# Decode work inside the linear layer's scan: split one-pass spreads, q as narrow weights, a new order at the end

## The chip, the cores and the metric

The kernel runs on one NeuronCore of a Trainium2 chip. Time is device microseconds of one launch; a kernel's time is the median of its runs. All arithmetic is in fp32, either by full fp32 products or by products of parts in the one-pass format fp32r.

## The reference

One inference step of a two-layer decoder with 512 prompt tokens and 8 decode sequences of one token each. Layer 0 mixes tokens by gated linear attention, layer 1 by native sparse attention; each is followed by a squared-relu MLP. The change lies in layer 0's mixer. For each of 4 heads (key width 128, value width 256) and, for the prompt, in chunks:

```python
S_new = jnp.exp(b_last[:, :, 0, :, None]) * S + jnp.einsum('bhck,bhcv->bhkv', kc * jnp.exp(b_last - b), vc)
o = o_inter + jnp.einsum('bhij,bhjv->bhiv', a, vc)
...
o = rms_norm(o, g_out).reshape(B, T, GLA_DV_TOT).astype(h.dtype)
return (o * jax.nn.silu(r)) @ w_out, s
```

For a decode sequence b this is: S'[b,h] = decay * S[b,h] + k[b,h] v[b,h] (an outer product), o[b,h] = q[b,h] S'[b,h]; o is normed over its 256 values, gated and projected. The updated states are outputs too.

## The kernel before, in words

Each engine runs its own hand-written sequence and waits on semaphores: TensorE (PE) for products, VectorE (DVE), ScalarE (ACT), GpSimd (POOL), and SyncE (SP) for loads. Activations lie transposed, model dimension on partitions. Dense projections are split products (`split_products`, L2066): weight and activation are each a high part that ACT copies out and a rest that DVE or POOL subtracts, and three fp32r products make one. A plain fp32 product shows as two records in the trace, an fp32r one as one.

After the input projection the scan follows. Its order is the list `GLA_STEPS` (L472), which every engine walks through, each taking the steps that are its own; a digit is the head, for `vb` the decode sequence. For the prompt: `kt` transposes decayed keys, `at` makes the chunk's triangular scores (32 small products, 64 records, after a bf16 product that zeroes the bank), `u` the states' increments (DVE then chains four states), `o` the outputs, `sq` squares them on ACT, `om` takes their mean on PE, `nr` makes root (ACT), reciprocal, two scalings (DVE) and the gate product (POOL, for the last head DVE). `da`, `xp`, `db` make the decay factors of heads 2 and 3 on DVE, ACT and POOL, `xq`, `dq` those of the queries; `st` stores the final prompt state.

Decode work is woven in by `vb`. The 2 x 2 MB of old states lie in the weight ring (`s0`). For sequence b, ACT scales four states by their decay (L1148), PE spreads the 1024 values of b over all 128 partitions by a product with a selector of 8 rows (L2172, two fp32 products of 512 columns), and DVE adds key times spread value to each state (L1607). Ahead of each `vb` but the first PE makes the outputs of the sequence before (`decode_out`, L2112 to L2121): eight fp32 products with a 128x128 piece of the state as weight and q as one moving column (L2118). The results lie in bank 1 of slot 3.

PSUM has four slots of two banks, handed out in the order of the list `product` (`at` and `omd` slot 3, `u` slot 0, `o` slot 1; `kt`, `om` and `vb` slot 2). Who claims a slot waits until the one before in it was read. After the list come the last decode output, the decode squares (L1156, L1157), their mean (`omd`, L2185) and root (L1162), then DVE's last gate product (L1623), the decode scalings (L1627), the decode gate product and the decode rest (L1633), for which the first output product waits; beside this POOL makes rests of output weights (L809) and of heads (L814) as ACT delivers the high parts (`out_weights_high` L1097, `out_high` L1103). POOL also stores the new states, four sequences at a time (L836); SP loads each half of the output weights after that store and after `od_full`.

## Time and profile before

| | us |
|---|---|
| median of 3 runs | 1972.5 (1971.04 to 1978.53) |
| profiled execution | 1968.85, of which the span 1967.1 |
| scan, first `kt` to first output product | 212.7 to 337.5 |
| TensorE busy over the span | 1790.7 (91%) |
| mean granted TensorE clock | 0.946 |

The page shows one execution. The clock is a share of 2.4 GHz; it is 1.0 or 0.5 at a time, and a value between is a mean. In the timelines and the chain, x counts records. The chain of waits is followed back from the last instruction; a piece with an engine and a line is work, a piece with q its sequencer.

### The profile page before, as it was taken

What the parts mean: (1) busy time and instruction counts of PE and PEld (TensorE: products, weight loads), DVE (VectorE), ACT (ScalarE), POOL (GpSimd) and SP (SyncE); (2) the same over time, 40 slices, a digit from 0 to 9 for tenths busy, and PEclk for the clock granted to TensorE, in tenths of its full rate; (3) what the DMA queues carried; (4) which work ended last, traced back from release to release, by engine and by line L of the source; (5) the groups of instructions that cost most, each with busy time, mean ns of one, the idle gap of its engine ahead of it and who ended that gap; (6) DMA issues with size and microseconds to landing.
All of it is one profiled execution on the core that took longest, in us unless ns stands there. A gap on an engine that the chain in (4) does not pass through costs nothing.

```text
span 1967.1 us, 32578 instructions
## 1 busy us (share of the span) xinstructions
PE 1790.7 (91%) x13592; PEld 1626.9 (83%) x13592; DVE 895.2 (46%) x1347; ACT 678.4 (34%) x1131; POOL 446.3 (23%) x381
## 2 busy tenths in 40 slices
PE   4999997999999997999799998898877999999996
PEld 2989876999999997989677786676644999999996
DVE  6051254744444345446622523877422644434343
ACT  3353233332313232323233422777641332313230
POOL 3244224100000002334212221787702100000000
PEclk9999777999999998999899999899987999999998
DMA  4122122223222221241221210001463322222211
GB/s 161 44 86 86 46 85 95 96 87 116 89 87 87 87 87 50 75 143 63 80 92 54 86 54 1 1 1 44 171 258 129 129 86 87 86 87 86 87 44 44
DMA packets 22254, 166.26 MB, mean 85 GB/s; under 512 B 2112, under 2 KB 9840, under 8 KB 12568
## 3 DMA queue, kind: packets, MB, share of 16 engines
q1 hardware_dynamic: 17896, 122.60, 16.7%
q0 software_dynamic: 4208, 41.45, 5.7%
q8 instruction: 120, 1.97, 0.4%
q14 instruction: 30, 0.25, 0.0%
HBM read 154.00 MB, written 10.04 MB: 83 GB/s over the span
## 4 chain that ended last, share of the span: by engine, by line
PE 79%; DVE 9%; ACT 5%; issue 3%; DMA 2%; POOL 1%; ACTq 0%; DVEq 0%; SPq 0%; PEldq 0%; POOLq 0%
PE slot L2066 53%; PE slot L2297 9%; PE slot L2038 2%; PE slot L2280 2%; ACT phase L1374 2%; PE slot L2140 1%; POOL phase L923 1%; DVE normed_x L1485 1%; PE slot L2172 1%; PE slot L2101 1%; DVE phase L1469 1%; PE slot L2426 1%; PE slot L2397 1%; PE slot L2118 1%; PE slot L2382 1%
## 5 line engine op out<-in xcount | busy, mean ns | idle before, releaser
L1198 ACT ACTIVATE w_high<-weights 128x1024 fp32r<-128x1024 f32 x128 | 135.3, 1060 | 258.1 <-PE slot L2066 250.0
L2066 PE MATMUL slot<-h_high,w_high 128*128 128x260 f32 x1024 | 210.5, 287 | 12.1 <-issue 12.1
L2066 PE MATMUL slot<-h_high,w_rest 128*128 128x260 f32 x1024 | 209.0, 286 | 2.8 <-issue 2.8
L2066 PE MATMUL slot<-h_rest,w_high 128*128 128x260 f32 x1024 | 208.8, 286 | 0.0
L2066 PE MATMUL slot<-u_high,w_high 128*128 128x260 f32 x1024 | 206.3, 283 | 0.0
L2066 PE MATMUL slot<-u_rest,w_high 128*128 128x260 f32 x1024 | 206.0, 283 | 0.0
L2066 PE MATMUL slot<-u_high,w_rest 128*128 128x260 f32 x1024 | 205.9, 283 | 0.0
L1665 DVE TENSOR_TENSOR w_rest<-weights,w_high 128x1024 fp32r<-128x1024 f32 x128 | 156.1, 1222 | 31.1 <-ACT w_high L1198 31.1
L2066 PEld LDWEIGHTS slot<-h_high,w_high 128*128 128x128 f32 x1024 | 160.7, 192 | 10.7 <-issue 10.3
L2066 PEld LDWEIGHTS slot<-h_rest,w_high 128*128 128x128 f32 x1024 | 160.5, 192 | 5.7 <-issue 5.7
L2066 PEld LDWEIGHTS slot<-h_high,w_rest 128*128 128x128 f32 x1024 | 160.3, 191 | 0.0
L865 POOL TENSOR_TENSOR pw_rest<-weights,pw_high 128x1024 fp32r<-128x1024 f32 x20 | 48.0, 2401 | 485.7 <-ACT pw_high L1181 469.1
L2066 PEld LDWEIGHTS slot<-u_rest,w_high 128*128 128x128 f32 x1024 | 157.8, 188 | 0.0
L2066 PEld LDWEIGHTS slot<-u_high,w_rest 128*128 128x128 f32 x1024 | 157.8, 188 | 0.0
L2066 PEld LDWEIGHTS slot<-u_high,w_high 128*128 128x128 f32 x1024 | 157.6, 188 | 0.0
L923 POOL TENSOR_SCALAR phase<-phase 128x128 f32<-128x128 f32 (+3 forms) x128 | 140.5, 1115 | 45.0 <-DVE phase L1478 44.9
L1685 DVE TENSOR_TENSOR phase<-phase 128x520 f32<-128x520 f32 x64 | 44.9, 701 | 202.3 <-ACT phase L1229 202.3
L1689 DVE TENSOR_TENSOR phase<-slot,base 128x520 f32<-128x520 f32 x64 | 44.8, 700 | 186.3 <-PE slot L2066 186.3
L1229 ACT ACTIVATE phase<-slot 128x520 f32<-128x520 f32 x64 | 38.8, 607 | 259.4 <-PE slot L2066 259.4
L2297 PE MATMUL slot<-xt_high,w_high 128*128 128x512 f32 x256 | 107.9, 421 | 4.7 <-DVE xt_rest L1799 4.7
L1799 DVE TENSOR_TENSOR xt_rest<-slot,xt_high 128x512 fp32r<-128x512 f32 (+1 forms) x80 | 48.9, 611 | 134.0 <-ACT xt_high L1305 133.2
L2297 PE MATMUL slot<-xt_rest,w_high 128*128 128x512 f32 x256 | 102.0, 398 | 0.0
(370 smaller groups left out, 3804.6 us busy)
## 6 DMA issues: line engine op xcount, KB each, us to landing
weights<-in_wt SPq DMA_DIRECT2D x47, 2048.0 KB, 8.5
weights<-in_state SPq DMA_DIRECT2D x2, 2048.0 KB, 8.6
out<-weights POOLq DMA_DIRECT2D x2, 2048.0 KB, 8.8
weights<-in_w SPq DMA_DIRECT2D x2, 2048.0 KB, 8.8
phase<-in_v_win SPq DMA_DIRECT2D x4, 1024.0 KB
out<-phase SPq DMA_DIRECT2D x6, 512.0 KB, 9.3
phase<-in_x_prompt SPq DMA_DIRECT2D x2, 1024.0 KB, 6.3
weights<-in_k_win SPq DMA_DIRECT2D x2, 1024.0 KB, 7.1
```

The costliest lines, as they stand in the source:

```text
L865: nc.gpsimd.tensor_tensor(pw_part[n % 2][1][:, :, :], ring[:, t % 2, :, 128 * (n % 4):128 * (n % 4) + 128], pw_part[n % 2][0][:, :, :].bit ...
L923: last = nc.gpsimd.tensor_scalar(rows, rows, small[:, 8 * (n % 4) + 6 + a:8 * (n % 4) + 7 + a], None, ALU.mult)
L1198: nc.scalar.activation(w_part[k % 4][0][:, :, :], ring[:, s, :, 128 * (k % 4):128 * (k % 4) + 128], ACT.Copy).then_inc(w_high_ready, 1)
L1374: ins_ = nc.scalar.activation(pst[:, n % PST, a, 0:w], scores[:, a, :], ACT.Exp, scale=HD ** -0.5, bias=small[:, 8 * (n % 4) + a:8 * (n % ...
L1665: nc.vector.tensor_tensor(w_part[k % 4][1][:, :, :], ring[:, s, :, 128 * (k % 4):128 * (k % 4) + 128], w_part[k % 4][0][:, :, :].bitcast(F ...
L1685: nc.vector.tensor_tensor(u, u, u, ALU.mult).then_inc(usq_ready, 1)
L1689: nc.vector.tensor_tensor(halves(gx), tok(ps), halves(rstd_sq), ALU.mult).then_inc(scale_ready, 1)
L1799: nc.vector.tensor_tensor(xt_part[1][:, sp % 2, 0:w], ps[:, 0, 0:w], xt_part[0][:, sp % 2, 0:w].bitcast(F32), ALU.subtract).then_inc(xt_re ...
L2038: last = mm(ps[0:weights(k).shape[1], a, 0:HT], weights(k), moving(k)[:, HT * a:HT * a + HT], start=k == 0, stop=k == chunks - 1)
L2066: last = mm(ps[0:w.shape[2], a, 0:HT], w[:, k, :], m[:, k, HT * a:HT * a + HT], start=k == 0 and w is high and m is x_high, stop=k == DC - ...
L2280: last = nc.tensor.transpose(ps[:, 0, nr * h:nr * h + nr], st2[0:nr, sp % 2, 128 * h:128 * h + 128], ident[0:nr, 0:nr])
L2297: last = mm(psh[:, c, 0:KV * nr], w1_part[wp][:, 8 * half + sp, 128 * c:128 * c + 128], xt_part[xp][:, sp % 2, half:half + KV * nr], start ...
```

## The change

- The spread of decode values: ACT writes the decode values to a buffer `gvd` and then their high part as fp32r to rows 0 to 7 of `gvd_part`, DVE the rest to rows 32 to 39; the selector holds ones for both, is loaded with 40 rows to `sel_in` and copied to fp32r by POOL. `vb` is then two fp32r products with 40 rows of contraction.
- The decode outputs: `qm` holds, for head h and sequence b, an 8-column weight in which only column b is q. A product with the whole 256 columns of state (h, b) adds row b of head h's outputs, in partitions 32h to 32h+7 of the bank, over all eight sequences. That is four fp32 products for a sequence, behind one wait for all its heads. The bank is zeroed by one more bf16 product at the first `at`.
- Since outputs now lie as rows, `dd` copies them out on ACT, `dt` transposes them on PE, ACT copies and squares them, `dm` is their mean, root, reciprocal, scalings and gate product. These steps stand in the list; `omd` and the work behind the list go.
- The order: `vb4` to `vb7` come earlier, ahead of `nr1`, `st2`, `u3` and `sq2`; `dd` follows `om2`, `dt` `nr2`, `dm` `o3`.
- The stores of the new states go from POOL's queue to SP's. POOL gets two memsets at its start.

```diff
--- before.py
+++ after.py
@@ -177,11 +177,16 @@
...
         wgr = carve("wgr", DC * RANK).rearrange("p (c n) -> p c n", n=RANK)
-        sel = carve("sel", NS * 128)[0:NS, :].rearrange("b (s p) -> b s p", s=NS)
+        carve("sel", NS * 128)
...
         osq = carve("osq", 2 * NP).rearrange("p (v t) -> p v t", v=2)
+        qm = carve("qm", GH * NS * NS).rearrange("p (h x) -> p h x", h=GH)
+        od_rows = carve("od_rows", DV)
+        osq_d = carve("osq_d", 2 * GH * NS)
+        rstd_d = carve("rstd_d", GH * NS)
+        gvd = carve("gvd", D)[0:NS, :]
@@ -194,6 +199,9 @@
...
+        sel_part = part("sel_part", at["sel"][0], NS, 128)[0:40, :, :]
+        sel_in = cols("qe", 0, NS * 128)[0:40, :]
+        gvd_part = part("gvd_part", at["gv"][0] + 4 * D, D)
@@ -472,12 +480,11 @@
...
                       "o0 vb1 u1 xq2 dq2 sq0 om0 nr0 vb2 da3 xp3 st1 "
-                      "o1 kt2 at2 db3 vb3 u2 xq3 sq1 om1 nr1 kt3 at3 dq3 vb4 st2 "
-                      "o2 vb5 u3 sq2 om2 nr2 vb6 st3 o3 sq3 om3 vb7 nr3").split()]
+                      "o1 kt2 at2 db3 vb3 u2 xq3 sq1 om1 vb4 nr1 kt3 at3 dq3 vb5 st2 "
+                      "o2 vb6 u3 vb7 sq2 om2 dd0 nr2 dt0 st3 o3 dm0 sq3 om3 nr3").split()]
         for what, n in GLA_STEPS:
-            if what in ("kt", "at", "u", "o", "om", "vb"):
-                product((what, n), {"at": 3, "u": 0, "o": 1}.get(what, 2))
-        product("omd", 3)
+            if what in ("kt", "at", "u", "o", "om", "vb", "dt", "dm"):
+                product((what, n), {"at": 3, "u": 0, "o": 1, "dm": 3}.get(what, 2))
@@ -684,7 +691,7 @@
...
             sp.dma_start(gw2, ins["gw2"]).then_inc(gla_small_in, 16)
-            sp.dma_start(sel.rearrange("b s p -> b (s p)"), ins["sel"]).then_inc(gla_small_in, 16)
+            sp.dma_start(sel_in, ins["sel"]).then_inc(gla_small_in, 16)
@@ -695,6 +702,9 @@
...
             for g in range(2):
+                sp.wait_ge(s0_new, GH * NS // 2 * (g + 1))
+                sp.dma_start(outs[3].rearrange("l b h k v -> k (l b) h v")[:, 4 * g:4 * g + 4, :, :],
+                             s0[:, 4 * g:4 * g + 4, :, :]).then_inc(s0_out[g], 16)
@@ -771,6 +781,8 @@
...
             nc.gpsimd.memset(cols("zerosb", 0, 256), 0.0).then_inc(bf_ready, 1)
+            nc.gpsimd.memset(gvd_part[:, :].bitcast(F32), 0.0).then_inc(bf_ready, 1)
+            nc.gpsimd.memset(cols("qm", 0, GH * NS * NS), 0.0).then_inc(bf_ready, 1)
@@ -800,6 +812,9 @@
...
                 gla_weights_rest(n)
+                if n == 4:
+                    pool.wait_ge(gla_small_in, 48)
+                    nc.gpsimd.tensor_copy(sel_part[:, :, :].rearrange("b s p -> b (s p)"), sel_in).then_inc(bf_ready, 1)
@@ -831,10 +846,6 @@
...
                         out_rest(1)
-                elif what == "vb" and n % 4 == 3:
-                    pool.wait_ge(s0_new, GH * (n + 1))
-                    pool.dma_start(outs[3].rearrange("l b h k v -> k (l b) h v")[:, n - 3:n + 1, :, :],
-                                   s0[:, n - 3:n + 1, :, :]).then_inc(s0_out[n // 4], 16)
@@ -1001,7 +1012,7 @@
...
-            act.wait_ge(bf_ready, 3)
+            act.wait_ge(bf_ready, 5)
@@ -1068,7 +1079,7 @@
...
                 ps, fr = await_product(act, ("gv", n))
-                dst = gv[0:rows, t, 256 * (n // 5):256 * (n // 5) + 256]
+                dst = (gv[:, t, :] if t < TT else gvd)[:, 256 * (n // 5):256 * (n // 5) + 256]
@@ -1086,6 +1097,8 @@
...
                     exps_key(n // 9)
+                elif n == 19:
+                    nc.scalar.activation(gvd_part[0:NS, :], gvd, ACT.Copy).then_inc(gv_ready, 1)
@@ -1103,6 +1116,14 @@
...
+            def root_d():
+                ps, fr = await_product(act, ("dm", 0))
+                nc.scalar.activation(rstd_d, ps[:, 0, 0:GH * NS], ACT.Sqrt, bias=eps_col).then_inc(root_ready, 1)
+                roots[0] += 1
+                act.wait_ge(root_ready, roots[0])
+                act.sem_inc(fr, 1)
@@ -1120,8 +1141,23 @@
...
                     nc.scalar.activation(go[:, 2 * h:2 * h + 2, 0:NP], ps[:, :, :], ACT.Copy).then_inc(go_ready, 1)
-                    act.wait_ge(go_ready, h + 1)
+                    act.wait_ge(go_ready, h + 1 + (h == GH - 1))
                     act.sem_inc(fr, 1)
+                elif what == "dd":
+                    act.wait_ge(od_full, 2)
+                    nc.scalar.activation(od_rows, slot[3][:, 1, 0:DV], ACT.Copy).then_inc(ogd_ready, 1)
+                elif what == "dt":
+                    ps, fr = await_product(act, ("dt", 0))
+                    od = ps[:, 0, 0:DV].rearrange("p (v h x) -> p h v x", v=2, h=GH)[:, :, :, 0:NS]
+                    nc.scalar.activation(go[:, :, NP:T].rearrange("p (h v) b -> p h v b", v=2), od, ACT.Copy)\
+                        .then_inc(go_ready, 1)
+                    nc.scalar.activation(osq_d.rearrange("p (v h b) -> p h v b", v=2, b=NS), od, ACT.Square)\
+                        .then_inc(osq_ready, 1)
+                    act.wait_ge(go_ready, GH)
+                    act.wait_ge(osq_ready, GH)
+                    act.sem_inc(fr, 1)
+                elif what == "dm":
+                    root_d()
@@ -1150,21 +1186,9 @@
...
             out_high(2)
-            act.wait_ge(od_full, 2)
-            od = slot[3][:, 1, 0:DC * NS].rearrange("p (b c) -> p c b", b=NS)
-            nc.scalar.activation(go[:, :, NP:T], od, ACT.Copy).then_inc(go_ready, 1)
-            nc.scalar.activation(osq[:, 0, 0:DC * NS].rearrange("p (c b) -> p c b", b=NS), od, ACT.Square)\
-                .then_inc(osq_ready, 1)
-            ps, fr = await_product(act, "omd")
+            act.wait_ge(ogd_ready, 2)
+            nc.scalar.activation(go_part[0][:, :, NP:T], go[:, :, NP:T], ACT.Copy).then_inc(heads_high_ready, 1)
             out_weights_high(2)
-            act.wait_ge(on_ready, GH)
-            nc.scalar.activation(rstd[:, 0:GH * NS], ps[:, 0, 0:GH * NS], ACT.Sqrt, bias=eps_col).then_inc(root_ready, 1)
-            roots[0] += 1
-            act.wait_ge(root_ready, roots[0])
-            act.sem_inc(fr, 1)
-            act.wait_ge(ogd_ready, 1)
-            nc.scalar.activation(go_part[0][:, :, NP:T], go[:, :, NP:T], ACT.Copy).then_inc(heads_high_ready, 1)
@@ -1587,6 +1611,12 @@
...
                 decay_queries(h)
+            dve.wait_ge(gv_ready, 21)
+            nc.vector.tensor_tensor(gvd_part[32:32 + NS, :], gvd, gvd_part[0:NS, :].bitcast(F32), ALU.subtract)\
+                .then_inc(gv_ready, 1)
+            dve.wait_ge(bf_ready, 5)
+            dve.wait_ge(gz_ready, GH)
+            nc.vector.tensor_copy(qm[:, :, 0:NS * NS:NS + 1], gq[:, :, NP:T]).then_inc(gv_ready, 1)
@@ -1616,19 +1646,19 @@
...
                     last.then_inc(on_ready, 1)
-            scale = rstd[:, 0:GH * NS]
+                elif what == "dm":
+                    reciprocal_root(rstd_d)
+                    by_head = go[:, :, NP:T].rearrange("p (h v) b -> p h v b", v=2)
+                    for v in range(2):
+                        last = nc.vector.scalar_tensor_tensor(by_head[:, :, v, :], by_head[:, :, v, :], P("gla_g")[:, v:v + 1],
+                                                              rstd_d.rearrange("p (h b) -> p h b", b=NS), ALU.mult, ALU.mult)
+                    link(last)
+                    nc.vector.tensor_tensor(go[:, :, NP:T], go[:, :, NP:T], gr[:, :, NP:T], ALU.mult).then_inc(ogd_ready, 1)
...
             nc.vector.tensor_tensor(o_last, o_last, r_last, ALU.mult).then_inc(og_last_ready, 1)
-            reciprocal_root(scale)
-            by_head = go[:, :, NP:T].rearrange("p (h v) b -> p h v b", v=2)
-            for v in range(2):
-                last = nc.vector.scalar_tensor_tensor(by_head[:, :, v, :], by_head[:, :, v, :], P("gla_g")[:, v:v + 1],
-                                                      scale.rearrange("p (h b) -> p h b", b=NS), ALU.mult, ALU.mult)
-            link(last)
-            nc.vector.tensor_tensor(go[:, :, NP:T], go[:, :, NP:T], gr[:, :, NP:T], ALU.mult).then_inc(ogd_ready, 1)
@@ -2106,17 +2136,15 @@
...
-            pe.wait_ge(bf_ready, 3)
-            pe.wait_ge(gv_ready, 20)
+            pe.wait_ge(bf_ready, 6)
+            pe.wait_ge(gv_ready, 23)
...
+                pe.wait_ge(s0_new, GH * b + GH)
                 for h in range(GH):
-                    pe.wait_ge(s0_new, GH * b + h + 1)
-                    for v in range(2):
-                        n = DC * b + 2 * h + v
-                        last = mm(slot[3][:, 1, n:n + 1], s0[:, b, h, 128 * v:128 * v + 128], gq[:, h, NP + b:NP + b + 1],
-                                  start=True, stop=True)
+                    last = mm(slot[3][32 * h:32 * h + NS, 1, 0:DV], qm[:, h, NS * b:NS * b + NS], s0[:, b, h, :],
+                              start=False, stop=b == NS - 1, skip_group_check=True)
@@ -2133,6 +2161,8 @@
...
                     mm(ps[:, 0, :], identb, zerosb, start=True, stop=False, skip_group_check=True)
+                    if h == 0:
+                        mm(ps[:, 1, :], identb, zerosb, start=True, stop=False, skip_group_check=True)
@@ -2169,21 +2199,29 @@
...
                     for a in range(2):
-                        last = mm(ps[:, a, :], sel[:, h, :], gv[0:NS, TT, 512 * a:512 * a + 512], start=True, stop=True)
+                        last = mm(ps[:, a, :], sel_part[:, h, :], gvd_part[0:40, 512 * a:512 * a + 512], start=True, stop=True)
+                    last.then_inc(fu, 1)
+                elif what == "dd":
+                    decode_out(NS - 1)
+                elif what == "dt":
+                    ps, fu = claim(pe, ("dt", 0))
+                    pe.wait_ge(ogd_ready, 1)
+                    for v in range(2):
+                        last = nc.tensor.transpose(ps[:, 0, 128 * v:128 * v + 128], od_rows[:, 128 * v:128 * v + 128], ident)
+                    last.then_inc(fu, 1)
+                elif what == "dm":
+                    pe.wait_ge(osq_ready, GH)
+                    ps, fu = claim(pe, ("dm", 0))
+                    for v in range(2):
+                        last = mm(ps[:, 0, 0:GH * NS], C("mean_v"), osq_d[:, GH * NS * v:GH * NS * v + GH * NS],
+                                  start=v == 0, stop=v == 1)
...
                 elif what == "om":
-                    pe.wait_ge(osq_ready, h + 1)
+                    pe.wait_ge(osq_ready, h + 1 + (h == GH - 1))
...
                     last.then_inc(fu, 1)
-            decode_out(NS - 1)
-            pe.wait_ge(osq_ready, GH + 1)
-            ps, fu = claim(pe, "omd")
-            squares_d = osq[:, 0, 0:DC * NS].rearrange("p (h v b) -> p h v b", v=2, b=NS)
-            for v in range(2):
-                last = mm(ps[:, 0, 0:GH * NS], C("mean_v"), squares_d[:, :, v, :], start=v == 0, stop=v == 1)
-            last.then_inc(fu, 1)
@@ -2560,9 +2598,10 @@
...
     parts.append(np.where(end[None, None, :] <= q[:, :, None], 0, NEG).astype(np.float32).reshape(128, -1))
-    sel = np.zeros((NS, NS, 128), np.float32)
+    sel = np.zeros((40, NS, 128), np.float32)
     sel[np.arange(NS), np.arange(NS)] = 1
-    return np.concatenate(parts, 1), sel.reshape(NS, -1)
+    sel[np.arange(NS) + 32, np.arange(NS)] = 1
+    return np.concatenate(parts, 1), sel.reshape(40, -1)
...
```

## Rows read from the trace of the kernel before

**Rows 1.** The page, its part on the chain that ended last, by engine.
```profile
PE 79%; DVE 9%; ACT 5%; issue 3%; DMA 2%; POOL 1%; ACTq 0%; DVEq 0%; SPq 0%; PEldq 0%; POOLq 0%
```

**Rows 2.** Windows over the scan: length, busy us of each engine, granted clock, DMA share.
```profile
213.00:338.00 125.00, 112.16 (x602) 87.15 (x600) 63.67 (x96) 46.83 (x74) 39.52 (x31) 0.71 0.24 81
```

**Rows 3.** Chain of waits from 205 to 345 us: start us, us, engine, line, records.
```profile
by line: PE slot L2140 18.5%; PE slot L2172 14.9%; PE slot L2118 10.8%; PE slot L2066 10.7%; PE slot L2149 9.1%; PE slot L2160 8.7%; PE slot L2178 6.3%; PE slot L2163 6.1%; DVE phase L1616 4.4%; DVE base L1469 2.6%; PE slot L2129 1.7%; DVE 
...
219.95 3.71 PE slot L2172 x4
...
241.47 1.68 PE slot L2118 x16
243.15 2.15 PE slot L2172 x4
...
248.62 1.72 PE slot L2178 x4
...
278.95 6.88 PE slot L2140 x64
285.83 3.39 PE slot L2118 x16
...
299.36 1.91 PE slot L2172 x4
...
303.19 1.93 PE slot L2178 x4
...
337.48 7.61 PE slot L2066 x51
```

**Rows 4.** Timeline of TensorE, 1441 to 1450 us: start, us, engine, line, operation, tiles.
```profile
1442.09 1.07 PE L2457 MATMUL slot<-phase 128*32 128x512 f32 x8
1443.08 1.97 PE L2426 MATMUL slot<-base,weights 128*128 128x128 f32 x16
```

**Rows 5.** Line L2486: ns min/median/max, first and last start, forms.
```profile
L2486 PE MATMUL slot<-phase x160: 374/379/636, 1476.9 to 1503.8; 128*32 128x256 f32 x128, 63*32 63x256 f32 x16, 8*32 8x256 f32 x16
```

**Rows 6.** Chain of waits over the whole span, products of split parts.
```profile
969.65 2.81 PE slot L2297 x12
```

**Rows 7.** Timeline of ScalarE from 195 to 345 us.
```profile
244.88 1.04 ACT L1126 ACTIVATE phase<-phase 128x1024 f32<-128x1024 f32 x1
...
267.02 0.60 ACT L1112 ACTIVATE normed_x<-slot 128x512 f32<-128x512 f32 x1 [0.18 <-ACT phase L1122]
```

**Rows 8.** Timeline of VectorE from 195 to 345 us; in brackets idle time before.
```profile
219.99 0.69 DVE L1564 TENSOR_TENSOR normed_x<-slot,base 128x512 f32<-128x512 f32 x1 [64.29 <-PE slot L2140]
...
251.39 3.35 DVE L1469 RECIPROCAL base<-base 128x512 f32<-128x512 f32 x1
...
256.11 1.65 DVE L1607 SCALAR_TENSOR_TENSOR weights<-slot,phase,weights 128x256 f32<-128x256 f32 x4
...
303.69 1.51 DVE L1578 SCALAR_TENSOR_TENSOR normed_x<-normed_x,phase,slot 128x256 f32<-128x256 f32 x3
...
328.44 6.11 DVE L1616 SCALAR_TENSOR_TENSOR phase<-phase,base 128x512 f32<-128x512 f32 x2
334.59 1.23 DVE L1623 TENSOR_TENSOR phase<-phase 128x1024 f32<-128x1024 f32 x1
```

**Rows 9.** Timelines of GpSimd (POOL), 0 to 112 and 100 to 345 us.
```profile
63.47 2.40 POOL L790 TENSOR_TENSOR gw_rest<-weights,gw_high 128x1024 fp32r<-128x1024 f32 x1 [3.35 <-ACT gw_high L1014]
...
266.02 6.99 POOL L782 TENSOR_TENSOR phase<-phase 128x64 f32<-128x64 f32 x8 [6.84 <-ACT phase L1052]
...
319.99 0.58 POOL L823 DMA_DIRECT2D out<-normed_x  x1
...
328.70 2.34 POOL L814 TENSOR_TENSOR go_rest<-phase,go_high 128x1024 fp32r<-128x1024 f32 x1
331.00 2.33 POOL L809 TENSOR_TENSOR gw_rest<-weights,go_w_high 128x1024 fp32r<-128x1024 f32 x1
```

**Rows 10.** The page, DMA issues: KB each, us to landing.
```profile
out<-weights POOLq DMA_DIRECT2D x2, 2048.0 KB, 8.8
```

## The prediction

> **What bounds the kernel now.** I read the page's chain first: TensorE (PE) carries 79% of it, so what is worth time is what PE does or waits for [rows 1]. The change touches one stage, the linear layer's scan from 213 to 337.5 us. Its windows show PE at work for 112.2 of 125 us, the granted clock 0.71 on average, so it runs somewhat longer at 1.2 than at 2.4 GHz [rows 2]. The chain of this stage stays on PE from the first `at` to 323 us; then it goes over DVE (the last state update, the last head's norm) until the output projection starts at 337.48 [rows 3]. The reader is to see two different stages: up to `om3` time is TensorE's instructions, behind it none of them.
>
> Two lines of it are what the change attacks: L2118, the decode outputs (16 records a sequence, two for each fp32 product), and L2172, the spread values (4 records). For one sequence they take 1.68 us at full clock and 3.39 at half, and 1.91 and 3.71 [rows 3]. Of the 140 us of that view the first has 10.8%, 15.1 us, and off the chain some 3.5 more for the seventh sequence, hidden beside DVE's update; the second has 14.9%, 20.9 us: 39.5 us in all.
>
> **Prices of the new products.** Decode outputs: 4 products in place of 8, an 8-column weight in place of 128, 256 moving columns, each head in its own quarter of the output's partitions. The nearest rows are 32-column weights with 512 moving columns, four quarters side by side: eight records start at 1442.09, the next wide transposes at 1443.08, so 0.99 us at full clock [rows 4]. Of that 2 x 0.43 is streaming by length; half the columns make 0.43, and with the 0.13 left over 0.56, at half clock 1.0. The wait for the updated state is now one for all four heads, behind which the first three queue; updates of the sequence before are long done. Bounds: nothing on the path where another engine is awaited, and 8 records in turn at 374 to 634 ns of one such record [rows 5], 3.0 to 5.1 us. I take 0.56 and 1.0, since the nearest row has the same four-quarter form.
> Spread values: two products of split parts. Split parts with 512 columns run 12 in 2.81 us [rows 6], 0.234 each, so 0.47, at half clock 0.9. The contraction is 40 rows in place of 8; 8 rows (L2172) and 128 (L2297) stream a column at the same rate, so I charge nothing for it; the other end is the old 1.91. A pair (decode output and spread) is then 1.03 or 1.9, 1.4 at the mean clock, where it was 3.6 to 7.1.
> The Trainium skill (TensorEngine Tiling (Array Packing), Key Properties) says that changing the tiling mode, not just the tile, drains TensorE. The change makes 16 such switches. The trace agrees that a switch costs something, but the 0.13 us above holds both of a visit's two; the rule names no price, and rival 5 has it as a mechanism.
>
> **The sum, in four stretches**, each against the chain before [rows 3].
> A, first `at` to start of `om0` at 248.62. The first spread goes from 3.71 to 0.9: -2.8. The second pair ran 1.68 and 2.15 and would fall to 1.2, but `om0` also needs ScalarE (ACT), which after `o0` copies, scales four states, makes an exponential and squares: it ended 245.92, 4.45 after `o0`'s end at 241.47 [rows 3, 7]. PE would be there 1.2 + 3.3 = 4.5 after it, 3.3 being the state product up to 248.62. No wait yet: -2.65. A: **-5.4**.
> B, `om0`'s end (250.34) to the start of the last `at` (278.95): 28.6. Were PE alone in question, four products less would save 10. But the rows of DVE and ACT show a chain of equal length: root, reciprocal 3.35, scaling, state update (ends 257.8, 7.4 after `om0`) [rows 8], exponents, ACT's exponentials, its copy of `o1`, its copy of `kt2` to 267.62, 17.3 after [rows 7]. Nothing of this moves earlier. PE now meets it three times. `kt2` writes slot 2, which DVE frees at +7.4: PE, there at +6.2, waits 1.2. `vb3` waits for `kt2`'s copy at +17.3, where PE would be at +15. Then 0.7 spread, 2.8 `u2`, 2.7 `om1` (`om0` took 1.72 at full clock; such products double at half, so about 2.7), root 0.7, spread 0.8, to +25.0; and because `vb4` now lies ahead of `kt3` in slot 2, `kt3` waits for its state update, 1.65 [rows 8]: +26.7, transposes and zeroing 0.8: +27.5. B: **-1.1**. POOL's 6.99 us of key decays, done at 273.0 [rows 9], is 22.7 after `om0`, not last.
> C, last `at` to start of `om2` at 303.19: 24.2. Out go 3.39 + 3.71 + 1.68 + 1.91 = 10.7; in come two pairs, 2.8. Then a new wait: `vb7` lies ahead of `om2` in slot 2, DVE does the head's states first (a copy and 1.51, about 2.0) and the update 1.65 after [rows 8], with hand-overs 3.9 after `u3`; the third pair lies inside. C: -10.7 + 2.8 + 3.9 = **-4.0**.
> D, `om2` to the output projection: was 34.3. The last decode products, their squares, mean and root now lie ahead of `o3` and `om3`, so the 6.4 us of the last update pair and the 1.8 us of small decode steps behind the norm leave the end. What is late next is POOL. From `om2`'s start: `om2` 2.7, decode output 0.8, ACT's copy of its rows 0.45 and root 0.75 (4.7); DVE reciprocal and scaling 4.8 (9.5); POOL's product 2.34, three more of 2.34, its store's issue 0.58 (19.4), three more: 7.0 (26.4) [rows 9]. DVE's scaling of the last head needs POOL to stop: in the trace the same two instructions took 6.11 us where two normally take 1.4, because POOL ran without a pause until 333.33; they ended 1.22 after it [rows 8, 9]. So +1.22, product 1.23 [rows 8], decode rest and hand-over 0.5: 29.4. D: **-4.9**. The small decode scalings on DVE are held up by POOL's first burst as well, which ends ahead of the second.
> The Trainium skill (SBUF - State Buffer, SBUF: two separate sides) calls the port pair shared by the two engines an exclusive lock, held by whichever starts first for its whole instruction. The scalings began at 328.44 and were not through before two POOL instructions were, so here DVE waited for more than the one instruction that the rule allows; by the rule it would get in after one, which is the tail rival below.
> Sum: -5.4 - 1.1 - 4.0 - 4.9 = **-15.4 us**.
>
> **What I cost at nothing.** Two more memsets on POOL: it idles from about 1 us until 21. The split of the selector: a POOL copy of at most 2.4 us, in one of the pauses of 3.35 us between weight blocks of 2.40 [rows 9]. 128 KB more for it in front of the weight tiles: under 0.5 us, and weights wait for ACT there. DVE's two small instructions for the split values and the spread-out q lie where it idles 64.29 us [rows 8]. ACT's one (about 1 us of 1024 columns) precedes the gate products, between which it is mostly idle. With no cover each would cost its length, some 4 us together. The states' stores leave POOL's queue for SP's, where they lie ahead of the waits for the output weights' tiles. The second can now start by about 295, its tile lands some 17 us later (twice the 8.8 of the old store [rows 10]), and its first use is the fifth output product, at about 345: hidden.
>
> The profiled execution took 1968.85 us (span 1967.1), 3.65 under the median 1972.5 of runs from 1971.04 to 1978.53. A profile after should show about 1953.5, the median **1957**.
>
> **Rivals.** (1) TensorE's gain arrives whole: 39.5 - 11 = 29 in the scan and 5 behind it, 1939. For it: the chain is nearly all PE. Against it: the three waits of B and the one of C, read from order and rows. (2) The clock. If the shortened, oftener interrupted PE sits at 1.2 GHz for three quarters of the scan rather than a half, its remaining 80 us of work (112 less some 31) grow by about 13, of which the waits swallow half: 1963.5; at a quarter, 1951.5. Low stretches follow the `at` products and waits; but some also follow the one-column products that go. (3) The tail: POOL lets DVE in after one instruction each: the norm ends some 4 us sooner, 1953. (4) The narrow products don't run side by side: 8 x 0.21 = 1.7 us at full clock, as before; it counts where PE is last, 5 of 8 visits: 1963 to 1966. (5) Slower: every record drains before the next and at each switch, 374 to 634 ns a record, mean 5 us with half clock [rows 5]: 8 x 4.2 = 34 over my price, most of it on the path, with 8 of it swallowed by waits: 1983. It turns the sign from a decode output of 2.7 us on (15.4 / 8 over my 0.8). Against it: the 0.99 us for eight records.
>
> **Numbers.** Forecast 0.50 (its own range 1951 to 1962), (1) 0.12, (2) slow side 0.18, (3) 0.10, (4) 0.06, (5) 0.04. Range 1945 to 1966: it holds (2) to (4) and the faster half between forecast and (1). Half a per cent is 9.9 us, about what a measurement of this kernel tells from none. Under 1962.6 lie the forecast, (1), (3) and 0.07 of (2): faster 0.79; same 0.11 + 0.06 = 0.17; slower 0.04.
>
> **What would show it.** A decode output of 0.5 to 1.0 us and a spread of 0.5 to 0.9 on PE; new PE idle ahead of `kt2`, the second state product, `kt3` and the third `om`; the last scalings ending about 1.2 us behind POOL; the output projection starting near 322; everything behind it shifted and unchanged. A narrow product over 2 us, or no waits on PE, would prove me wrong, one on each side.

## The result and the profile after

The changed kernel takes 1940.5 us (median, 1938.35 to 1941.27) beside 1974.9 for the kernel before (1971.04 to 1978.53): ratio 0.9824, 95% interval 0.9801 to 0.9848. I had forecast 1957, at lowest 1945. The gain is 34 us in the medians and 27.9 in the profiled spans (1967.1 to 1939.2), where 15.4 were forecast. The direction was right, the size outside my range. The profiled execution of the kernel before was a quick one (1968.85 us, 6 under the median), so the account by stages below is of the 27.9 us alone.

The chain by engine and the window over the scan answer to [rows 1] and [rows 2].

```profile
PE 78%; DVE 10%; ACT 6%; issue 2%; DMA 2%; POOL 1%; ACTq 0%; DVEq 0%; SPq 0%; PEldq 0%; POOLq 0%
```

```profile
213.00:338.00 125.00, 96.11 (x572) 74.63 (x577) 73.39 (x98) 48.45 (x76) 39.54 (x30) 0.71 0.26 89
```

TensorE is at work 16 us less in that window and the mean granted clock is the same, 0.71. The window hides two things: it holds 8 us of the output projection more, and the clock of a stretch changed though the mean did not. The chain of waits of the changed kernel, 205 to 335 us (start, us, engine, line, records), answers to [rows 3]:

```profile
243.99 2.00 PE slot L2223 x4
...
254.75 9.11 PE slot L2170 x64
263.86 0.97 PE slot L2146 x8
264.84 1.15 PE slot L2202 x2
...
275.85 8.50 PE slot L2170 x64
...
299.80 2.85 PE slot L2223 x4
...
310.21 4.07 DVE phase L1654 x2
314.30 2.30 DVE phase L1657
316.60 3.27 DVE base L1493
319.90 7.64 DVE phase L1646 x2
327.57 1.22 DVE phase L1661
329.07 5.94 PE slot L2096 x26
```

The output projection begins at 329.07 where it began at 337.48: the scan gives 8.4 us, half of the forecast. So the forecast was too large in the stage that it worked out, and nearly 20 us came from places it never looked at. The chain names them. The feed-forward stages have 3072 products on line L2096 (L2066 before). In the changed kernel the chain over the whole span shows each as one unbroken piece:

```profile
381.73 369.11 PE slot L2096 x3072
1549.28 369.13 PE slot L2096 x3072
```

In the kernel before each is broken twice. From its chain of 560 to 780 us:

```profile
559.92 15.00 PE slot L2066 x125
574.91 1.55 issue
576.47 1.58 PE slot L2066 x11
578.04 1.35 issue
579.40 92.53 PE slot L2066 x757
671.93 1.54 issue
```

"issue" is time for which the profile knows no reason: no semaphore, no data. From first to last product these two stages took 378.5 and 383.1 us before and 369.2 and 369.2 after, 23.3 us less. The scan gives 8.4, and 3.8 are given back, 0.9 by a slower start of the output projection and 3.0 by the attention stages: 27.9 in all. These 3.0 I don't take for an effect of the change: the stages from the first feed-forward stage's end to the second's start took 792 to 800 us in all fourteen profiles, in no order that follows an edit.

What differs at those breaks is in the page's table of DMA queues (packets, MB, share), the row for instructions, first the kernel before, then the changed one:

```profile
q8 instruction: 120, 1.97, 0.4%
```

```profile
q8 instruction: 83, 1.36, 0.3%
```

37 packets less, of 16.4 KB each. Asked for 560 to 770 us, the DMA view counts 19 such packets in the kernel before and none in the changed one. The stage's last three panels are a loop in TensorE's program, of 1578 instructions a turn (768 products with a weight load each, and 42 others), with two jumps back per stage; the breaks stand at these jumps. After each jump some 9 of the packets come one after another over the whole next turn, so all of the loop is fetched again. The record of the jump itself is 3.5 to 3.8 us long in the kernel before and 0.2 in the changed one. The four jumps account for 20.9 of the 23.3 us (turns of 95.7 to 98.8 us for 92.3). The other 2.4 lie ahead of the first jump: the first 4 us of the two stages ran at a mean granted clock of 0.67 and 0.63 before and of 1.0 after. That part changes from profile to profile, and stages without a stall take 369.2 to 370.7 us.

The change touches no instruction of the loop. But it makes TensorE's program 153 instructions shorter ahead of it (fp32 products run as two records each, and there are fewer), so the loops lie elsewhere among the 16 KB pieces in which the program is fetched.

The Trainium skill (Runtime: NRT & Kernel Launch, Instruction fetch mechanics) says that instructions are refilled in blocks of 16 KiB, 256 instructions, and that a taken branch whose target is outside "the current 2-page window" forces a fetch and stalls. The trace agrees on the block (16.4 KB a packet) and on the stall, but not on the window: the changed kernel jumps back over six blocks without a fetch. That gave theory P: 1578 is six blocks and 42 instructions, so a turn touches seven blocks or, from 41 of the 256 starting positions, eight. With seven nothing is fetched again; with eight TensorE stalls at each jump.

### The profile page after: what moved, and what is told of

Read it like the earlier page. It is cut to its first block, busy times and chain, and to the rows that moved or that the text cites. A ratio compares the mean times of both kernels' runs of the same rounds, so it can differ in the third digit from the quotient of the medians.

```text
span 1939.2 us, 32429 instructions
## 1 busy us (share of the span) xinstructions
PE 1763.0 (91%) x13510; PEld 1603.5 (83%) x13515; DVE 905.0 (47%) x1349; ACT 679.6 (35%) x1133; POOL 444.8 (23%) x382
## 4 chain that ended last, share of the span: by engine, by line
PE 78%; DVE 10%; ACT 6%; issue 2%; DMA 2%; POOL 1%; ACTq 0%; DVEq 0%; SPq 0%; PEldq 0%; POOLq 0%
PE slot L2096 53%; PE slot L2335 9%; PE slot L2068 2%; PE slot L2318 2%; ACT phase L1398 2%; PE slot L2170 2%; DVE normed_x L1509 1%; POOL phase L934 1%; PE slot L2435 1%; PE slot L2131 1%; PE slot L2464 1%; DVE phase L1493 1%; PE slot L2420 1%; ACT phase L1412 1%; DVE base L1493 1%
## 5 line engine op out<-in xcount | busy, mean ns | idle before, releaser
L2096 PE MATMUL slot<-h_high,w_high 128*128 128x260 f32 x1024 | 206.7, 283 | 0.0
L2096 PE MATMUL slot<-h_high,w_rest 128*128 128x260 f32 x1024 | 206.5, 283 | 0.0
L2096 PE MATMUL slot<-u_high,w_high 128*128 128x260 f32 x1024 | 206.4, 283 | 0.0
L2096 PE MATMUL slot<-h_rest,w_high 128*128 128x260 f32 x1024 | 206.3, 283 | 0.0
L2096 PE MATMUL slot<-u_rest,w_high 128*128 128x260 f32 x1024 | 206.1, 283 | 0.0
L2096 PE MATMUL slot<-u_high,w_rest 128*128 128x260 f32 x1024 | 206.1, 283 | 0.0
L2096 PEld LDWEIGHTS slot<-h_high,w_high 128*128 128x128 f32 x1024 | 157.9, 188 | 0.1
L2096 PEld LDWEIGHTS slot<-h_high,w_rest 128*128 128x128 f32 x1024 | 157.8, 188 | 0.0
L2096 PEld LDWEIGHTS slot<-u_high,w_rest 128*128 128x128 f32 x1024 | 157.8, 188 | 0.0
L2096 PEld LDWEIGHTS slot<-u_rest,w_high 128*128 128x128 f32 x1024 | 157.8, 188 | 0.0
L2096 PEld LDWEIGHTS slot<-u_high,w_high 128*128 128x128 f32 x1024 | 157.6, 188 | 0.0
L2096 PEld LDWEIGHTS slot<-h_rest,w_high 128*128 128x128 f32 x1024 | 157.6, 188 | 0.0
L2335 PE MATMUL slot<-xt_high,w_rest 128*128 128x512 f32 x256 | 101.7, 397 | 0.0
```

The lines of the kernel that those rows point to most:

```text
L2096: last = mm(ps[0:w.shape[2], a, 0:HT], w[:, k, :], m[:, k, HT * a:HT * a + HT], start=k == 0 and w is high and m is x_high, stop=k == DC - ...
L2335: last = mm(psh[:, c, 0:KV * nr], w1_part[wp][:, 8 * half + sp, 128 * c:128 * c + 128], xt_part[xp][:, sp % 2, half:half + KV * nr], start ...
```

## The experiments

Times are medians; each group has its own runs of the kernel before (1970.3, 1972.5, 1970.2 us). "Scan" is first `at` to first product of the output projection; FF0 and FF1 are first to last product of the two feed-forward stages, where 369.2 to 370.7 is a stage without a stall; positions count the kernel's own instructions ahead of each loop, modulo 256.

```
kernel                    us      ratio (95%)             scan   FF0    FF1    positions
before                    1974.9  1                       124.0  378.5  383.1  170 191
after                     1940.5  0.9824 (0.9801-0.9848)  114.7  369.2  369.2   17  38
e1  after + 158 empty     1955.8  0.9914 (0.9881-0.9948)  111.2  380.5  370.3  175 196
e2  after + 220 empty     1950.5  0.9883 (0.9845-0.9922)  112.1  369.2  370.6  237   2
e3  before + 60 empty     1954.0  0.9909 (0.9877-0.9940)  127.2  369.2  369.2  230 251
e4  after + 128 empty     1952.9  0.9888 (0.9847-0.9930)  114.8  369.2  379.0  145 166
e5  before + 5 empty      1962.9  0.9954 (0.9932-0.9975)  127.3  381.5  370.4  175 196
e6  fp32 spreads          1946.9  0.9866 (0.9837-0.9895)  121.9  370.7  370.7   49  70
e7  other slots           1930.4  0.9787 (0.9756-0.9817)  106.7  370.6  369.2   17  38
e8  POOL held back        1933.4  0.9797 (0.9769-0.9826)  111.8  370.7  370.6   17  38
e9  POOL held longer      1932.8  0.9814 (0.9789-0.9839)  106.6  370.4  370.4   17  38
e10 slots and e9          1923.6  0.9767 (0.9741-0.9794)  102.1  370.7  369.2   17  38
e11 e10, earlier burst    1925.5  0.9764 (0.9741-0.9787)   99.9  370.7  370.3   17  38
e12 after + 138 empty     1955.8  one run                 114.7  373.9  381.3  155 176
```

### Where the loops lie: e1 to e5 and e12

All have the same edit, with N = 158, 220, 128, 138 on the changed kernel and 60 and 5 on the kernel before; `idle` is a semaphore that nobody waits for.

```diff
+            for _ in range(N // 2):
+                pe.sem_inc(idle, 1)
             pe.wait_ge(ident_in, 32)
...
             mean_square(0)
+            for _ in range(N - N // 2):
+                pe.sem_inc(idle, 1)
```

e1. 

> The changed kernel with 158 empty instructions (an increment of a semaphore that nobody waits for) put into TensorE's program at two places where TensorE idles in the first 60 us, so that the two loops of the feed-forward stages stand as far into TensorE's program as they did in the kernel before. Theory P (position of the loops): the body of 1578 instructions straddles one 256-instruction page more, is fetched again at each turn, TensorE stalls at four turns, and the 22.8 us that the two feed-forward stages gained go again: stage lengths about 381 and 383 us, time 1963. Rival Q (the stages run faster because of what the scan does differently: clock, memory traffic, buffers): the stages stay at 372 and 369 us, time 1940.

Half of it came. FF0 stalls again at both jumps, FF1 not. From the chain of e1:

```profile
568.05 1.77 issue
...
1559.75 370.02 PE slot L2101 x3072
```

The time also holds 5.5 us by which the scan starts later. I had thought TensorE idle at the two places, but in its records the empty instructions start 0.15 us apart: the first 79 run from 0.8 to 12.8 us, where the first transposes had begun at 7.0, and the other 79 from 28.3 to 40.5. Q is out: the scan of e1 is that of the changed kernel, and FF0 is slow.

e2. 

> As the run before, with 220 empty instructions. Theory P: the loops start shortly behind a page border again, the body fits into seven pages, no stall at the turns: stages of 372 and 369 us, time 1940. Rival R (more instructions ahead of the loops are what brings the stalls, wherever the page borders lie): 1963 or more.

No stall, though it has the most instructions ahead: R is out. The time is not 1940, since the start comes 9.8 us later; that is the padding's own price.

e3. 

> The kernel before, nothing of the change, with 60 empty instructions at the same two idle places. Theory P: the loops slip over a page border, the stalls at the four turns go, time 1974 - 23 = 1951 and the scan as long as before. Rival Q: 1974, both feed-forward stages at 381 and 383 us.

As theory P said (1954.0, both stages 369.2, scan 127.2). This is the kernel before, without its stalls. Beside it the changed kernel is 13.4 us faster in the medians, and 17 by the two ratios, each to its own group's kernel before; e3 starts its scan 2.5 us late by its padding, which has to come off. So without the stalls the change is worth some 11 to 14 us, a little under the 15.4 of the forecast; e3's ten times spread over 22 us (1944.4 to 1966.0), so this can't be said more closely.

e4. 

> The changed kernel with 128 empty instructions. 
e5. 

> The kernel before with five empty instructions in TensorE's program ahead of the loops. Theory P in its sharp form: counted over all runs so far, a loop stalls when it starts at position 166 to 191 of a 256-instruction page (by the count of the kernel's own instructions), and not at 2 to 145 or 196 to 251. Five more put the first loop at 175 (stalls stay, stage about 380 us) and the second at 196 (no stall, 369 us): time 12 us under the kernel before, 1959. Rival: only the rough distance matters, or the layout of other engines' programs: both stages as before, 1971.

Five instructions that do nothing take the stalls out of the second stage (383.1 to 370.4) and leave them in the first (381.5). From the chain of e5:

```profile
578.15 1.53 issue
...
1570.22 370.10 PE slot L2071 x3072
```

The kernel is faster by 9.5 us (ratio 0.9954, interval below 1), less than the 12 expected. In the profile the second stage alone gives 12.7; the scan and the first feed-forward stage were 3 us longer each.

e12. 

> The changed kernel with 138 empty instructions: the first loop starts at position 155 of a page, the second at 176. Theory P says that a body of 1578 instructions (six pages and 42) touches an eighth page for 41 of the 256 positions; the last that stalls lies between 191 and 195 by the runs so far, so the first between 151 and 155: both loops stall, stages of 379 to 383 us each. Rival (another width): the first stage 369 us, as at position 145.

At 176 both jumps stall (381.3). At 155 only the first of two does: its turn takes 96.9 us, the next 92.3, as a free one. So the lower edge lies above 145 and at or near 155, where a width of 41 puts it (the bounds alone allow 37 to 50), and at 155 the outcome is mixed, which theory P does not say. This rests on one run.

### Where the scan's gain went: e6 and e7

The timeline of TensorE in the changed kernel (start, us, line; in brackets idle time and what ended it) shows the new prices and the new waits:

```profile
239.42 0.62 PE L2146 MATMUL slot<-weights,phase 128*8 128x256 f32 x8
239.97 0.73 PE L2202 MATMUL slot<-gvd_part,sel_part 40*128 40x512 f32 x2
...
253.31 1.09 PE L2157 MATMUL slot<-base,phase 128*128 128x128 f32 x4 [2.46 <-DVEq L1640]
254.75 9.11 PE L2170 MATMUL slot<-phase 128*16 128x16 f32 x64 [0.36 <-issue]
...
275.08 0.63 PE L2157 MATMUL slot<-base,phase 128*128 128x128 f32 x4 [1.90 <-DVEq L1640]
275.85 8.50 PE L2170 MATMUL slot<-phase 128*16 128x16 f32 x64
...
299.80 2.85 PE L2223 MATMUL slot<-phase,base 128*128 128x512 f32 x4 [2.93 <-DVEq L1640]
```

The waits are those of the forecast. What it lacks is the line under two of them: the third and fourth `at` took 9.11 and 8.50 us. The fourth took 6.88 before [rows 3], and the third, in the same chain of the kernel before:

```profile
259.53 5.41 PE slot L2140 x64
```

That is 5.41, for the same 64 records. Windows over just these products give the granted clock (the number before the DMA share), in the changed kernel

```profile
254.80:263.80 9.00, 9.00 (x65) 8.56 (x66) 3.26 (x9) 5.40 (x7) 2.45 (x5) 0.50 0.05 16
275.90:284.30 8.40, 8.40 (x67) 7.97 (x70) 3.88 (x3) 2.15 (x5) 2.87 (x2) 0.55 0.72 266
```

and in the kernel before, the third `at` (the fourth ran at 0.74 there):

```profile
259.60:264.90 5.30, 5.30 (x65) 5.00 (x64) 3.14 (x9) 2.13 (x3) 0.00 (x0) 1.00 0.07 25
```

With the new waits ahead of them, the third `at` ran at 1.2 GHz, where it had run at 2.4, and the fourth for nearly all its length, where it had run at 2.4 for about half.

e6.

```diff
-  last = mm(ps[:, a, :], sel_part[:, h, :], gvd_part[0:40, 512 * a:512 * a + 512], ...)
+  last = mm(ps[:, a, :], sel_part[0:NS, h, :].bitcast(F32), gvd[:, 512 * a:512 * a + 512], ...)
```

> The changed kernel with the spread values as before, fp32 products of 8 rows (1.91 us at full clock, 3.7 at half) in place of split ones of 40 rows (0.73 and 1.22). If a spread's price arrives where PE is last: of eight, those of the first head's stretch (2.5) and of om1's, at3's stretch (1.2 to 2.5 each) show in full, those behind a wait for slot 2 only in what exceeds the wait: 7 to 12 us more in the scan, time 1949. Rival (the scan is bound by DVE's and ACT's chain, waits swallow nearly all): 0 to 3 us, 1942.

6.4 us in the medians, 7.2 in the scan: about half of the difference in price (1.25 us at full clock, 2.6 at half, eight times) arrives, the other half is swallowed. The spread was worth its edit.

e7.

```diff
-  product((what, n), {"at": 3, "u": 0, "o": 1, "dm": 3}.get(what, 2))
+  product((what, n), {"at": 3, "u": 0, "o": 1, "dm": 3, "vb": {2: 0, 4: 0, 7: 1}.get(n, 2)}.get(what, 2))
```

> The changed kernel with three of the eight spread values written to other buffers of the accumulator memory (the third and fifth to slot 0, the eighth to slot 1, all others stay in slot 2), nothing else. If the new PE waits ahead of kt2 (2.46 us), kt3 (1.90) and the third om (2.93) are the price of sharing slot 2 with a spread that waits for DVE's update: they go, the third om then waits some 0.3 us for ScalarE, and with less half-clock time behind them the scan is 5 to 7 us shorter, time 1934. Rival (DVE's and ACT's chain of equal length stands behind them): the waits come back ahead of u2, at3 and o3, and the scan gains 0 to 2 us.

10.1 us in the medians (7 by the ratios) and 8.0 in the scan of the profile, more than the high end. Its TensorE timeline:

```profile
250.51 0.60 PE L2157 MATMUL slot<-base,phase 128*128 128x128 f32 x4
...
251.26 5.72 PE L2170 MATMUL slot<-phase 128*16 128x16 f32 x64
...
263.22 1.22 PE L2202 MATMUL slot<-gvd_part,sel_part 40*128 40x512 f32 x2 [5.27 <-ACTq L1136]
...
272.78 6.38 PE L2170 MATMUL slot<-phase 128*16 128x16 f32 x64
...
292.87 1.98 PE L2223 MATMUL slot<-phase,base 128*128 128x512 f32 x4 [0.34 <-ACT phase L1162]
```

The three waits are gone or fall to 0.34 us, and both `at` are short again (12.1 us for the two in place of 17.6), at a granted clock of 0.95 and 0.82. The 2.46 us come back, and more, ahead of a spread that waits for ScalarE's copy of `kt2`: there the chain of DVE and ACT that I had in stretch B binds. From first `at` to last `om` the stretch took 93.2 to 96.7 us in the seven kernels that kept the old slots and the split spreads, and 88.7, 88.6 and 88.8 in the three with the new slots. The rival has nothing but that one wait.

### The tail: e8, e9, e10, e11

In the changed kernel GpSimd runs from 309.58 to 326.3 with no pause (start, us, line):

```profile
318.78 0.58 POOL L838 DMA_DIRECT2D out<-normed_x  x1
319.38 2.35 POOL L824 TENSOR_TENSOR gw_rest<-weights,go_w_high 128x1024 fp32r<-128x1024 f32 x1
321.68 2.34 POOL L829 TENSOR_TENSOR go_rest<-phase,go_high 128x1024 fp32r<-128x1024 f32 x1
323.98 2.33 POOL L824 TENSOR_TENSOR gw_rest<-weights,go_w_high 128x1024 fp32r<-128x1024 f32 x1
```

DVE's last scalings (L1646) begin at 319.90 and take 7.64 us in place of 1.4, through 1.2 us behind GpSimd's stop, as forecast.

e8, in GpSimd's program:

```diff
-            out_weights_rest(1)
             out_rest(2)
+            pool.wait_ge(on_ready, GH)
+            out_weights_rest(1)
```

> The changed kernel with GpSimd's next weight remainder held back until DVE has scaled the last head (GpSimd does the third head's remainder first). If GpSimd's unbroken run is what makes DVE's last scalings take 7.6 us in place of 1.4: they start when GpSimd stops at about 321.7, end at 323.1, and the output projection starts at 324.8 in place of 329.1: scan 4 us shorter, time 1936. Rival (the scalings are slow for another reason, or something else is late next): output projection within 1 us of 329.

The scalings took 3.06 us and the last `om` to the output projection 15.65 instead of 18.05: 2.4 of the 4.3 us. The median moves by 7.1, more than the 2.9 by which its profiled scan is shorter; that profile is the slowest of e8's four executions (1938.7). GpSimd started again at once, beside the next DVE instruction, which then took 2.38 us for 0.22:

```profile
318.68 3.06 DVE L1647 SCALAR_TENSOR_TENSOR phase<-phase,base 128x512 f32<-128x512 f32 x2
321.76 1.22 DVE L1662 TENSOR_TENSOR phase<-phase 128x1024 f32<-128x1024 f32 x1
322.91 2.38 DVE L1664 TENSOR_TENSOR go_rest<-phase,go_high 128x64 fp32r<-128x64 f32 x1
```

e9: the wait is for DVE's last remainder, `pool.wait_ge(go_rest_ready["last_head"], 1)`, in place of `on_ready`.

> As the tail run, but GpSimd waits until DVE has made the last head's remainder too. There DVE's last two scalings took 3.06 us, and the decode remainder behind them, normally 0.22, took 2.38, because GpSimd had started again beside it. If it is GpSimd beside it that makes it slow: the decode remainder takes 0.22 again and the output projection starts 14 us behind the start of the last om in place of 15.65 (18.05 in the changed kernel): time 1935. Rival (the later weight remainder makes the second output product late): the same start, but the output projection gives the 2 us back, time 1937 or more.

13.5 us from the last `om`; the remainder is back at 0.22. The median does not move against e8 (1932.8 and 1933.4); of the 5.2 us that its profiled scan is shorter, 3.0 lie ahead of the last `om`, where the two programs are the same. The rival's price (a later second output product) does not show: from the output projection's first product to FF0 it is 51.3 us, and 52.3 in the changed kernel.

e10 is e7 and e9 together.

> Both edits, the other slots for three spreads and GpSimd held back at the tail. They act in different stretches, so they should add: 7.7 us from the slots up to the last om, 4 from the tail behind it, output projection at 317.5, time 1927.

They add, each in its own stretch: 88.6 us from the first `at` to the last `om` as in e7, 13.5 behind it as in e9, 102.1 us of scan. The time is 1923.6 us, 3 better than expected.

e11. Beside e10's edits:

```diff
                     if n == 2:
+                        pool.wait_ge(ogd_ready, 2)
                         out_weights_rest(0)
-                        out_rest(0)
-                        out_rest(1)
+                elif what == "dd":
+                    out_rest(0)
+                    out_rest(1)
```

and ScalarE's two `out_high` move from behind the third head's root to behind its square.

> As the run before, and GpSimd's earlier burst taken apart too: the remainders of heads 0 and 1 (with ScalarE's rounded copies that they need) are made before the third head's norm, and the first weight remainder only after DVE's decode scalings. If GpSimd's burst is what makes DVE's decode scalings (normally some 0.3 us each) take 6.35 us in all, and so delays the last reciprocal queued behind them: the output projection starts 12 us behind the start of the last om, at about 315, time 1925. Rival (ScalarE's copies, now earlier, delay the third om or the decode row copy): the stretch up to the last om grows by 2 us and the gain is gone.

In DVE's timeline of e11 the decode scalings and product take 2.14 us in place of 6.35, and the last reciprocal now waits for ScalarE, not for them:

```profile
302.48 1.91 DVE L1658 SCALAR_TENSOR_TENSOR phase<-phase,base 128x32 f32<-128x32 f32 x2
304.42 0.23 DVE L1661 TENSOR_TENSOR phase<-phase 128x64 f32<-128x64 f32 x1
307.05 3.35 DVE L1497 RECIPROCAL base<-base 128x512 f32<-128x512 f32 x1 [2.40 <-ACT base L1175]
```

From the last `om` it is 11.05 us, 2.4 less than in e10. The time does not show it: 1925.5 against 1923.6, intervals on top of each other. Its profile has 4.9 us more between the feed-forward stages, more than the tail gives. e10 and e11 are both faster than both kernels; which of them is the better one these runs can't say.

## Why the prediction was wrong

**The step that failed** stands in the last part of what the profile should show: "everything behind it shifted and unchanged". The sum had no term for anything behind the scan; there the two feed-forward stages took 23.3 us less, and the rest behind the scan gave 3.8 back, so 19.5 of the 27.9 us came from behind it. I had counted TensorE's instructions for their time and not for their place. The profile before had the sign. Its chain has 3% "issue" [rows 1], of which most lies elsewhere and stays (2% after), but the page's table of instruction groups puts 15 us of it on these very products, where the changed kernel has 0.0:

```profile
L2066 PE MATMUL slot<-h_high,w_high 128*128 128x260 f32 x1024 | 210.5, 287 | 12.1 <-issue 12.1
L2066 PE MATMUL slot<-h_high,w_rest 128*128 128x260 f32 x1024 | 209.0, 286 | 2.8 <-issue 2.8
```

I read over it. With theory P the stalls would have been found, though not the position without a trial, since the instructions ahead of the kernel's own are not in the profile.

**The scan** was forecast at 15.4 us and gave 9.3 from first `at` on. By stretches, against the chains of both profiles:

- A, forecast -5.4: 35.1 to 29.6, -5.5. That it agrees is in part luck. I had the state product at 3.3 us and no wait; it took 2.0 at the higher clock, and then TensorE waited 1.37 for ScalarE's square. Both ways `om0` starts 4.5 us behind `o0`'s end.
- B, forecast -1.1: 28.6 to 29.9, +1.3. The waits ahead of `kt2` and `kt3` were there, 2.46 and 1.90 for 1.2 and 1.65. The wait of `vb3` was not, because `at` before it ran 3.7 us longer and covered it; e7, with a short `at`, has it.
- C, forecast -4.0: 24.2 to 23.95, -0.3. The removed products went out and the wait for slot 2 came in at 2.93; `at` took 1.6 us more and the first products behind it ran at half clock too (1.2 us more than forecast on the pair and `o2`). From `o2`'s end to `om2`, with that wait in it, it was 0.8 more.
- D, forecast -4.9: 34.3 to 29.3, -5.0. POOL was late next, as said, and the scalings ended 1.2 us behind it. `om0` itself, which lies between A and B, took 0.3 us more.

So the mis-sized term is the clock in B and C, which are 6.1 us short of their forecast. The third `at` took 3.7 us more, of which 1.5 arrived, since the rest ran where TensorE would have waited for `kt2`'s copy; the spread and the state product behind it cost 1.4 more than forecast, `om1` 0.8 less. In C it is 1.6 on `at` and the 1.2 named above. That makes some 5 of the 6.1; this split is read off two chains and not tested apart. My rival 2 had the mechanism, new waits that lower the granted clock, and 6.5 us for it; I gave it as a case apart, when it belonged in the sum, since it comes behind the very waits that I forecast. That it works through these waits is what e7 shows: take the waits, and the `at` are short. In the three kernels with the new slots the two `at` took 5.6 to 6.4 us, in the seven with the old slots and the split spreads 7.7 to 9.1.

How far one profile can be trusted on this: with nothing changed in the scan, the kernel before took 124.0, 127.2 and 127.3 us for it in three profiles, the changed one 111.2 to 114.8 in five. The means are 12.7 apart, nearer to my 15.4 than the one pair is.

**The prices** held. Decode output 0.55 us from its start to the next instruction's at full clock and 0.97 at half (forecast 0.56, 1.0); spread 0.66 and 1.15 (forecast 0.47, 0.9, so low by 0.2). Rivals 4 and 5 are out by that. Rival 1 (all of TensorE's 29 us) is out though its time, 1939, is near the measured one: it would have had the output projection at about 303 and the stages behind it unchanged. A time that fits is no evidence without the stretch in which it should arise. Rival 3 (DVE gets in after one GpSimd instruction) is out for the last scalings; at the small ones it holds: two scalings and a product, which take 0.2 us each elsewhere, took 6.35 us in all and ended at 311.97, 314.27 and 316.60, each just behind one of GpSimd's instructions (311.92, 314.22, 316.52).

## What to carry to other kernels

Before a gain or loss is put down to an edit, compare the lengths of the stages that it does not touch; if a loop is among them, look at "issue" in the chain and at the instruction queue's packets, and try a few empty instructions in front. Price a new wait with what runs behind it at the lower clock, not with its idle time alone. A buffer shared by a product that waits for another engine and one that need not is a wait given away: three numbers in a table were worth 8 us of the scan here.

## What the runs showed of the hardware

- A loop of 1578 instructions on TensorE costs nothing at its jumps from ten of the positions tried (2, 17, 38, 49, 70, 145, 196, 230, 237, 251) and 8.2 to 12.7 us per stage of two jumps at 166, 170, 175, 176 and 191 (3.5 to 6.5 a jump); at 155 one jump of two cost 4.7. The blocks are 16.4 KB. A free turn is 92.3 us, one with a stall 95.7 to 98.8. That a turn touching eight blocks doesn't fit is the reading that these positions bear out, but for the one free jump at 155; where a block begins is fitted to them, and that the eighth block is what is missing was not seen directly.
- Some of DVE's instructions on SBUF took longer beside GpSimd's: the remainder 2.38 us for 0.22 (e8), two scalings 7.64 for 1.4. Updates from accumulator memory (1.65 for four, at 310.60 in the kernel before, beside GpSimd's product from 310.78 on) and the reciprocal (3.34 at 316.53 in the changed kernel) took their usual time beside it.
- Empty instructions are not free: the semaphore increments on TensorE start 0.15 us apart, though a record is 0.05 long. With 79 and 79 of them (e1) the first wide product came at 40.8 us instead of 32.0, with 110 and 110 (e2) at 50.0; with 30 and 30 (e3) they fitted into idle time, and it came at 31.9.
